# Two more modulation parts of the first layer formed on VectorE instead of TensorE

## What is computed

```python
c_act = silu(c)
for l in range(DEPTH):
    mod = c_act @ w_mod[l] + b_mod[l]                     # 1024 x 6144 weights, one row
    sh_m, sc_m, g_m, sh_f, sc_f, g_f = split(mod, 6)      # parts 0 to 5
    h = rms_norm(x, norm_mix_g[l]) * (1.0 + sc_m) + sh_m
    x = x + g_m * mixer(h, ...)       # three branches, gates, projections, w_out
    h = rms_norm(x, norm_ffn_g[l]) * (1.0 + sc_f) + sh_f
    x = x + g_f * moe_ffn(h, ...)     # 64 experts, 8 for each token, and a shared one
```

## Time and profile before

| | us |
|---|---|
| median of 3 runs | 2412.13 (2407.19 to 2412.92) |
| the profiled execution | 2415.04 |
| its span, first to last instruction | 2413.7 |

### The profile page before, as it was taken

The page is one execution under the profiler, slowest core; times in us unless marked ns, Lnnn a source line. Parts: engine busy times, 40 slices in busy tenths (PEclk is TensorE's granted clock), DMA queues, the critical chain, the costliest instruction groups (busy, mean ns, idle before and its releaser), DMA issues.

```text
span 2413.7 us, 34586 instructions
## 1 busy us (share of the span) xinstructions
PE 2312.0 (96%) x14027; PEld 1654.2 (69%) x14027; DVE 814.4 (34%) x2133; ACT 569.4 (24%) x1231; POOL 135.8 (6%) x179
## 2 busy tenths in 40 slices
PE   7999999999998988999999999998989999999998
PEld 4868896666665655768887676665657777754764
DVE  0376623222121211485524122111213534421264
ACT  2234402111111112134211111111113333321254
POOL 4040000000000000100000000000000000000110
PEclk9999999999999999999999999999999999999999
DMA  9785685999999997855776999999994453141300
GB/s 338 273 294 180 240 322 208 383 414 413 414 417 414 417 412 261 304 187 193 284 300 240 382 414 417 414 414 418 412 366 135 157 167 122 70 149 52 140 1 18
DMA packets 206907, 673.21 MB, mean 279 GB/s; under 512 B 14000, under 2 KB 74648, under 8 KB 156816
## 3 DMA queue, kind: packets, MB, share of 16 engines
q1 hardware_dynamic: 200064, 656.87, 70.5%
q0 software_dynamic: 6240, 13.99, 1.7%
q10 hardware_dynamic: 432, 0.01, 0.0%
HBM read 661.38 MB, written 9.45 MB: 278 GB/s over the span
## 4 chain that ended last, share of the span: by engine, by line
PE 83%; DMA 11%; ACT 2%; SPq 2%; DVE 1%; issue 1%; POOL 0%; DVEq 0%; ACTq 0%
PE ps L278 47%; PE ps L2166 11%; PE ps L2201 6%; DMA ring<-in_w 6%; DMA ar<-in_w 5%; PE ps L2217 3%; PE ps L1748 3%; SPq L570 1%; PE ps L1198 1%; PE ps L686 1%; PE ps L2895 1%; PE ps L3508 1%; DMA ring<-in_w_in 1%; PE ps L3656 1%; PE ps L3673 1%
## 5 line engine op out<-in xcount | busy, mean ns | idle before, releaser
L278 PE MATMUL ps<-hT,ring 128*128 128x256 f32 (+2 forms) x2352 | 542.8, 386 | 3.2 <-ACT ar L1568 1.9
L278 PEld LDWEIGHTS ps<-hT,ring 128*128 128x128 f32 (+1 forms) x2352 | 439.7, 190 | 100.2 <-issue 37.1
L2166 PE MATMUL ps<-ring,ar 128*32 128x256 f32 (+2 forms) x2752 | 315.6, 392 | 36.3 <-DMA ring<-in_w 25.0
L2166 PEld LDWEIGHTS ps<-ring,ar 128*32 128x32 f32 (+2 forms) x2752 | 191.1, 126 | 147.8 <-issue 59.0
L2166 PE MATMUL ps<-ar 128*64 128x256 f32 (+2 forms) x1104 | 206.3, 395 | 9.5 <-DMA ar<-in_w 8.0
L2491 DVE SCALAR_TENSOR_TENSOR exact_parts<-ps,ar,exact_parts 128x512 fp32r<-128x512 f32 x100 | 75.1, 751 | 254.9 <-ACT exact_parts L2335 249.2
L2201 PE MATMUL ps<-ring,ar 128*32 128x512 f32 (+2 forms) x680 | 150.0, 624 | 8.9 <-DMA ring<-in_w 8.9
L2166 PEld LDWEIGHTS ps<-ar 128*64 128x64 f32 (+2 forms) x1104 | 120.2, 134 | 33.2 <-issue 14.4
L2467 DVE TENSOR_TENSOR ar<-ar,ps 128x256 f32<-128x256 f32 x50 | 21.1, 421 | 356.1 <-PE ps L2166 356.1
L278 PE MATMUL ps<-ring,ar 128*128 128x512 f32 x320 | 139.8, 593 | 0.9 <-DVE ar L3737 0.9
L2335 ACT ACTIVATE exact_parts<-ps,ar 128x512 fp32r<-128x512 f32 x100 | 68.7, 687 | 232.7 <-PE ps L2201 214.5
(11 more groups left out here) (463 smaller groups left out, 2852.7 us busy)
## 6 DMA issues: line engine op xcount, KB each, us to landing
ring<-in_w SPq DMA_DIRECT2D x257, 1024.0 KB, 17.9
ar<-in_w SPq DMA_DIRECT2D x104, 1024.0 KB, 20.0
ring<-in_w_mod SPq DMA_DIRECT2D x36, 2048.0 KB, 12.3
ring<-in_w_in SPq DMA_DIRECT2D x28, 2048.0 KB, 11.9
ring<-in_ab_w_in SPq DMA_DIRECT2D x47, 1024.0 KB, 10.8
cst<-in_w SPq DMA_DIRECT2D x23, 1024.0 KB, 17.0
ring<-in_w_out SPq DMA_DIRECT2D x4, 2048.0 KB, 10.2
ring<-in_ab_w_out SPq DMA_DIRECT2D x2, 4096.0 KB, 12.9
```

Source lines behind the costliest of these rows:

```text
L278: ins = te.matmul(o, l, r, start=(first and i == 0), stop=(last and i == len(pairs) - 1), skip_group_check=lax)
L2166: ins = te.matmul(b[cols, 0:256], K.x_b[:, kk, in_pair(p, cols)], w[r][:, kk, :], start=(kk == 0), stop=(kk == 7))
```

## The change

Layer 0's parts 2 and 3 move from the early to the direct ones, at the head of the direct list: twelve half items instead of eight. The mod2 parts are placed behind "qc" and "qk". VectorE takes five items beside the branches instead of four. In the merge TensorE takes items 3 and 4 behind w_proj_a's products, 5 behind w_proj_b's, and 6 to 11 after blocks 0, 2, 4, 5, 6, 7 of the third gate; VectorE takes 5 with branch a's merges, 6 with branch b's, and 7 to 11 in one piece before branch c's. The load list follows. Layer 1 keeps its places.

```diff
-        gate(l, 1, ((2,), (3,)))
+        gate(l, 1, ((2,), (3, 4) if l == 0 else (3,)))
         for b, n in enumerate(("w_proj_a", "w_proj_b", "w_proj_c")):
             if b > 1:
-                gate(l, b, ((6,), (7,)))
+                gate(l, b, ((7, 8), (9, 10, 11)) if l == 0 else ((6,), (7,)))
             rows(("proj", l, b), I[n][l], 4, 2)
             if b < 2:
-                direct(l, (4 + b,))
+                direct(l, (4 + b + (l == 0),))
...
 def early_parts(l):
     if l == 0:
-        return [("mod", 0, 2), ("mod2", 0, 0), ("mod2", 0, 1), ("mod", 0, 3)]
+        return [("mod2", 0, 0), ("mod2", 0, 1)]
...
 def direct_parts(l):
-    return [("mod", 0, 4), ("mod", 0, 5), ("mod", 1, 0), ("mod", 1, 1)] if l == 0 else [("mod", 1, j) for j in range(2, 6)]
+    return [("mod", 0, j) for j in range(2, 6)] + [("mod", 1, 0), ("mod", 1, 1)] if l == 0 else [("mod", 1, j) for j in range(2, 6)]
...
-EARLY_AT = ("qc", "qk", "qk", "vc"), ("ua", "ug", "qc", "qk")
+EARLY_AT = ("qc", "qk"), ("ua", "ug", "qc", "qk")
...
-    yield from dve_direct(K, l, range(4))
+    yield from dve_direct(K, l, range(DIRECT_FIRST[l]))
 
 
 DIRECT_BESIDE = {(0, 5): (0,), (1, 1): (1,), (1, 5): (2,)}
-DIRECT_MERGE = {1: (5,), 4: (6,), 7: (7,)}
+DIRECT_FIRST = 5, 4
+DIRECT_PROJ = ((3, 4), (5,)), ((3,), (4,))
+DIRECT_MERGE = {0: (6,), 2: (7,), 4: (8,), 5: (9,), 6: (10,), 7: (11,)}, {1: (5,), 4: (6,), 7: (7,)}
...
-                yield from pe_direct(K, l, DIRECT_MERGE.get(k, ()))
+                yield from pe_direct(K, l, DIRECT_MERGE[l].get(k, ()))
...
-            yield from pe_direct(K, l, (3 + br,))
+            yield from pe_direct(K, l, DIRECT_PROJ[l][br])
...
-    yield from act_direct(K, l, (3, 4))
+    yield from act_direct(K, l, DIRECT_PROJ[l][0] + DIRECT_PROJ[l][1])
...
-    pieces = dve_direct(K, l, range(4, 8))
+    pieces = dve_direct(K, l, range(DIRECT_FIRST[l], 12))
...
-    yield from pool_direct(K, l, range(3, 8))
+    yield from pool_direct(K, l, range(3, 12))
```

More of the change, by code:

```diff
@@ L323, in memory @@
     K.landed = [K.sem(f"ring_landed{i}") for i in range(2 * UNITS)]
-    K.direct_kept = nc.dram_tensor("direct_kept", (8, D), F32).ap()
+    K.direct_kept = nc.dram_tensor("direct_kept", (10, D), F32).ap()
     K.s_direct, K.n_direct = [K.sem(f"direct_row_kept{n}") for n in range(3)], [0] * 3
@@ L713, in early_parts, with direct_items @@
     if l == 0:
-        return [("mod", 0, 2), ("mod2", 0, 0), ("mod2", 0, 1), ("mod", 0, 3)]
+        return [("mod2", 0, 0), ("mod2", 0, 1)]
     return [("mod2", 0, 2), ("mod2", 1, 0), ("mod2", 1, 1), ("mod2", 1, 2)]
 def direct_parts(l):
-    return [("mod", 0, 4), ("mod", 0, 5), ("mod", 1, 0), ("mod", 1, 1)] if l == 0 else [("mod", 1, j) for j in range(2, 6)]
-def direct_items(l, ns=range(8)):
+    return [("mod", 0, j) for j in range(2, 6)] + [("mod", 1, 0), ("mod", 1, 1)] if l == 0 else [("mod", 1, j) for j in range(2, 6)]
+def direct_items(l, ns=range(12)):
     items = [(*key, q) for key in direct_parts(l) for q in range(2)]
     return [items[n] for n in ns if n < len(items)]
-EARLY_AT = ("qc", "qk", "qk", "vc"), ("ua", "ug", "qc", "qk")
+EARLY_AT = ("qc", "qk"), ("ua", "ug", "qc", "qk")
 def early_at(l, place):
@@ L841, in pe_direct, with direct_at @@
         K.pe.also("used", *item)
+def direct_at(l, item):
+    return len(direct_items(0)) * l + direct_items(l).index(item)
 def direct_place(l, item):
-    return (8 * l + direct_items(l).index(item)) % 3
+    return direct_at(l, item) % 3
 def act_direct(K, l, ns):
     for item in direct_items(l, ns):
-        n = 8 * l + direct_items(l).index(item)
+        n = direct_at(l, item)
         K.ac.wait_ge(*(yield ("direct_ps", *item)))
@@ L1772, in act_merge @@
         ac.activation(K.sg[:, k, :], K.ps["gate_ps", l, 2, k][:, 0:256], ACT.Sigmoid).then_inc(*K.act("gate", l, 2, k))
-        yield from act_direct(K, l, DIRECT_MERGE.get(k, ()))
+        yield from act_direct(K, l, DIRECT_MERGE[l].get(k, ()))
 def dve_merge(K, l):
```

## The result

| | before | after |
|---|---|---|
| median of 20 runs each | 2412.36 us (2406.52 to 2414.65) | 2415.81 us (2412.42 to 2417.91) |
| the profiled execution | 2415.04 us | 2416.10 us |
| its span | 2413.7 us | 2414.8 us |
| mean TensorE clock | 0.987 | 0.987 |

The ratio of after to before is 1.0015, 95% interval 1.0009 to 1.0021: 3.5 us slower (2.2 to 5.1), where +2.0 (2414.1 us) was forecast. The slowdown is small, half of the 0.3% that the prediction took as telling something from no change, but the interval leaves no change out.

A forecast was written before the change was run, and what follows sets the result against it. It took TensorE as the bound (96% busy, 59.00 of 59 us in the merge), with late loads there stalling it. 5.64 us gained and 7.7 lost gave +2.0 on the median 2412.13: 2414.1 us, range 2407 to 2419.

The forecast's parts named there:

- rival (2): Slower loads in the merge: a spacing of 5.8 us holds, +3.5 us, 2415.6 us; chance 0.13.
- Removed, 7.07: Ahead of the branches: parts 2 and 3 leave TensorE, so the branches start 7.07 us earlier.
- Rival (4): Branch start doesn't move because VectorE's convolution ends as late as before: +5.1 us, 2417.2 us; chance 0.05.
- The fifth item, 0: Beside the branches: VectorE's extra item takes 6.0 us, its late merge start is made up, cost 0.
- Added on TensorE, 1.43: Four more half parts by matmuls with ones, 0.36 us each, cost 1.43 us.
- d6's load: Merge: the load of item 6, issued at 268.1, lands at 276.5; VectorE stands 8.4 us for it.
- TensorE waits for banks by under 1 us: In the ctx turns and first gate block, TensorE waits under 1 us for banks while branch b's merges run late.
- Load spacing of 5.5: Merge: from item 6 on, 2 MB loads land 5.5 us apart, item 9's at 304.0.
- The three waits, 7.7: Third gate: TensorE stalls at items 9, 10 and 11 for 3.4, 2.2 and 2.1 us, 7.7 lost.
- Behind it: After branch c's products start: w_out's halves land before they are wanted at 336.6; cost 0, up to 1 us.
- The clock, rival (3): From branch c's products on, stalls lower TensorE's granted clock: +3.8 to +5.6 us, 2415.9 to 2417.7; chance 0.10.
- VectorE's room, rival (1): Merge loads land early enough, only multiplications count: −1.5 us, 2410.6; with no stall −5.6, 2406.5; chance 0.14.

The follow-up runs named there:

- e1: Kernel before, TensorE multiplying parts 2 and 3 over 64 of 512 columns; the stage (first L686 stretch to branch c's products) takes 219.12 us, 5.60 less than before.
- e10: Kernel before, with TensorE's matmuls of parts 2 and 3 done twice; 2418.52 us against 2412.52, ratio 1.0022.
- e6: The change with one part instead of two: only part 3 moves, ten items; 2411.10 us against 2412.61 for before, ratio 0.999.
- e3: Changed kernel, VectorE doing 2 of the 8 instructions of items 7 to 11; the stage takes 225.44 us, 2.18 less than after.
- e8: Changed kernel with idle matmuls on TensorE ahead of its waits for items 9, 10 and 11; 2414.81 us against 2412.62 for before, ratio 1.0009.
- e2: Changed kernel, loads of items 9 to 11 bringing 64 bytes a partition instead of 16 KB; the stage takes 223.06 us, 4.56 less than after.
- e4: Changed kernel, TensorE taking item 3 beside the branches so item 6's load is issued some 14 us earlier; 2415.45 us against 2412.62 for before, ratio 1.0009.
- e5: e4 with item 5 behind branch a's products and item 9's load ahead of the second gate half; 2414.14 us against 2412.62 for before, ratio 1.0004.
- e9: e6 with item 3 taken beside the branches and items 4 and 5 behind branch a's products; 2406.24 us against 2412.62 for before, ratio 0.998.
- e12: The same kernel as e9, run once more; 2408.20 us against 2412.52 for before, ratio 0.998.

## Why the prediction came out as it did

The mechanism was right, and the sum was short by 0.9 of 2.9 us in the stage. The stage's +2.9 lies just inside the forecast's 0 to +3, the +3.5 of the medians just outside; by number alone rival (2), with +3.5, came closer. What ends the stage is the chain of d6's load, the loads behind it and VectorE's last three items, and its errors add up to the 0.9: d6 0.4 late, five load steps 0.7 longer, and three items that together took 0.2 less. In the order of the prediction's steps:

- *Removed, 7.07.* Measured 7.00 at the branches' first matmul (164.08, forecast 165.3 − 1.26 = 164.04). Rival (4) fell: the convolution moved with the first stretch, and its cover shrank to 0.39, forecast 0.4. e1 and e10 show that this time passes on to branch c's products.
- *The fifth item, 0.* Right: VectorE ends it at 254.8 (forecast 256.5 − 1.26), and branch a's products start 7.44 earlier. That is 0.37 more than removed. What gave it in the branches is not known; e6 gained 0.4 there too, and e1 lost 0.4.
- *Added on TensorE, 1.43.* Four more half parts at 0.36; d3 and d4, now in one place, take 0.58 together, so 1.29.
- *d6's load.* VectorE takes d6 at 275.60, forecast 276.5 − 1.26 = 275.2; branch b is merged at 287.5, forecast 287.2. Right, with two small errors against each other: the issue came 0.4 us earlier than forecast, and the load landed 9.1 us behind it instead of 8.4.
- *TensorE waits for banks by under 1 us.* From the context turns to the first gate block 3.20 us went by, before 289.40 to 291.29, so 1.31 are lost, more than the prediction's under 1 us. It cost nothing here, since TensorE came to d9 early all the same. It does cost where no item is late: e6 lost 0.8 by it.
- *Load spacing of 5.5.* From d6 to d9 5.64 in after and 5.67 in e3. This is the term that was mis-sized: five steps of 5.5 against 28.2 us are 0.7 of the 0.9. d9 was due at 302.7 by the forecast and came at 303.81. The mean lay between the forecast's and that of rival (2), 5.8. But e3 shows that the pace itself was right: from d8 on four loads come at 5.43 each, and the excess lies in the three behind d6, the first load into an empty queue, at 5.84 each. In the packets of after the queue has moved its first 2.1 MB by 274.2 and 2.1 MB more every 5.5 us, those of d9 by 301.8; VectorE starts on d6 1.4 us behind that, and on d9 2.0 behind. So the queue moved the bytes at the pace of the forecast, and what grew is the time from the bytes to the landing; why it grew isn't shown. The Trainium skill, "DMA: Bandwidth & Descriptors", section Specifications, has some 358 GB/s for one core. The rates measured here lie above it, and the measurement decides: 366 for the nine loads, 372 for the five steps of 5.64 (2.1 MB each), and 390 from 305 to 315.
- *The three waits, 7.7.* Block to block they are 3.39, 2.03 and 2.03 (309.95 − 303.04 − 3.52, and 5.55 − 3.52 twice), 7.45 in all.
- *Behind it.* w_out starts at 336.04, forecast 336.6 − 1.26 = 335.3, and isn't waited for. The stage's +2.9 lies within the interval of the whole, +3.5 (2.2 to 5.1).
- *The clock, rival (3).* Its event came, behind a wait of 3.19 us at 309.95, but inside the gate, where the wait for d10 covers it, as the prediction put it for such a place. It was not the cause of the stage's +2.9: e8 took it away and the stage stayed as long. Uncovered it costs: in e2 branch c's products took 1.7 us longer. The Trainium skill, "TensorE: Matmul & The Clock Gate", section HAM oscillation, has waits between bursts return the clock to half; for the gap of 2.2 us near 371 the traces bear that out in before and in e8 and not in after.
- *VectorE's room, rival (1).* It fell: e2 gives that room back by taking the bytes away, and of the kernels with twelve items it alone ends the stage below before (223.06 against 224.72: −1.7, where the prediction had −1.5 for VectorE alone).

What the prediction did not see is how deep the cause goes. It follows everything from d6's late load, and in after that is so: the full queue starts with it. But e4 shows that this is only the first of several such bounds. With d6 released early the hole moves behind it, to d8, held by branch b's products, and with that mended to d10, held by the first gate half (e5). In after the time is that of a full queue; in e4 and e5 it is that of a ring of five places that come free at TensorE's pace. One part fits into the stage (e6, e9, e12); two didn't in any of the three orders tried.

## What to carry to other kernels

An engine at a third of its time is not free room for work that needs 2 MB of loads for each item: lay out the loads between the moment from which they can be issued and the moment at which they are used, at the spacing that the trace shows for a full queue, before you count instructions. When one load is late, look for the next one in the ring before you take the first as the cause; here one edit removed a wait of 9 us and didn't move the end of the stage forward (e4), and one more removed two waits of over 4 us, brought one of 7 us, and moved it by 2 (e5). Half of such a change can be worth more than the whole: one part gave 2.0 us in the stage and two cost 2.9 (medians: 1.5 less and 3.5 more than before); with the earlier releases one part gave 3.25 and two cost 0.9 (medians: some 5 less, and 1.5 more, which its interval doesn't tell from no change).

## What the runs showed of the hardware

- A gap of TensorE doesn't always cost its clock. The gap of 2.2 us near 371 (363 to 376, as the kernels differ) is in all thirteen traces, ahead of the same work. A stretch at half clock followed it in four (before, e1, e3, e8: the 16 matmuls behind it took 5.3 us) and none in the nine others (3.64 us). The longer gaps of the stage, 3.19 to 3.34 us, were followed by one each time (after, e3, e4, e5).
- Two-megabyte loads in a full queue were spaced by 5.4 to 5.5 us (381 to 390 GB/s) from the fourth step of a run on, and by 5.8 over the first three steps, which follow an empty queue (e3), from landing to landing. The mean of the five steps from d6 to d9 didn't depend on how long VectorE worked on what had landed (5.67 in e3, 5.64 in after).
